# Moving a 31-tap depthwise convolution from between the triangular inverses to beside the in-projection

## What is computed

```python
z = h @ w_in                                             # h: 512 x 1024
c_in, q, k, v, zg, b_raw, a_raw, gate_c, gate_d = split_cols(z, IN_SPLITS)
# convolution branch: 512 channels
u = c_in[..., :CONV_WIDTH] * jax.nn.sigmoid(c_in[..., CONV_WIDTH:])
u = causal_depthwise_conv(u, conv_dw_w) + conv_dw_b      # 31 taps per channel
u = jax.nn.silu(layer_norm(u, conv_ln_gain, conv_ln_bias))
y_conv = u @ w_conv_out
# gated delta branch: 8 heads of 64
qkv = jax.nn.silu(causal_depthwise_conv(concat([q, k, v]), gdn_conv_w))   # 4 taps
...
o = gated_delta_rule(q, k, v, beta, g)   # per head and chunk: a triangular solve, then a scan over chunks
```

## Time and profile before

| | us |
|---|---|
| median of three runs | 974.13 |
| lowest, highest | 972.68, 975.51 |
| the profiled execution's own time | 975.37 |
| its span in the trace | 973.6 |
| PE busy | 852.3 (88%) |
| DVE busy | 644.9 (66%) |
| ACT busy | 491.2 (50%) |
| POOL busy | 357.1 (37%) |

### The profile page before, as it was taken

The page is one execution under the profiler, slowest core; times in us unless marked ns, Lnnn a source line. Parts: engine busy times, 40 slices in busy tenths (PEclk is TensorE's granted clock), DMA queues, the critical chain, the costliest instruction groups (busy, mean ns, idle before and its releaser), DMA issues.

```text
span 973.6 us, 11909 instructions
## 1 busy us (share of the span) xinstructions
PE 852.3 (88%) x4386; PEld 669.7 (69%) x4386; DVE 644.9 (66%) x778; ACT 491.2 (50%) x641; POOL 357.1 (37%) x241
## 2 busy tenths in 40 slices
PE   4999999578868979999999999399999999999950
PEld 3888877478758878885878456267777777777730
DVE  5499424979968964741116212758889888888836
ACT  7555430333424313244532113168888888888832
POOL 6254541575245602212564000223534435343110
PEclk9999999798979969999999998599999999999985
DMA  8563222000000021041080703749999998999406
GB/s 290 194 217 87 87 87 87 1 1 1 1 0 1 1 87 66 21 173 65 23 308 0 279 25 122 278 170 361 353 371 379 364 370 347 351 368 343 169 11 258
DMA packets 49818, 163.53 MB, mean 168 GB/s; under 512 B 11192, under 2 KB 15304, under 8 KB 41198
## 3 DMA queue, kind: packets, MB, share of 16 engines
q1 hardware_dynamic: 42398, 152.41, 41.6%
q0 software_dynamic: 7376, 10.52, 3.2%
HBM read 154.51 MB, written 25.17 MB: 185 GB/s over the span
## 4 chain that ended last, share of the span: by engine, by line
PE 54%; DVE 10%; DMA 2%; ACT 2%; POOL 1%; issue 1%; POOLq 0%; DVEq 0%; SPq 0%; ACTq 0%
PE bank L388 13%; PE bank L390 13%; PE bank L389 13%; PE bank L686 6%; DVE arena L1533 4%; PE bank L731 3%; DVE arena L1584 1%; DMA h_lo<-low_h 1%; DVE arena L1855 1%; PE bank L589 1%; DVE gu_lo L1681 1%; PE bank L627 1%; PE bank L609 1%; PE bank L526 1%; PE bank L753 1%
## 5 line engine op out<-in xcount | busy, mean ns | idle before, releaser
L1681 DVE TENSOR_TENSOR gu_lo<-wgu,gu_hi 128x2048 fp32r<-128x2048 f32 x64 | 146.4, 2289 | 21.8 <-ACT gu_hi L1325 21.5
L986 POOL TENSOR_TENSOR w_lo<-arena,w_hi 128x1024 fp32r<-128x1024 f32 x36 | 89.4, 2490 | 166.0 <-ACT w_hi L1113 166.0
L1325 ACT ACTIVATE gu_hi<-wgu 128x2048 fp32r<-128x2048 f32 x64 | 122.1, 1909 | 19.0 <-DMA h2T_keep<-arena 10.1
L1533 DVE SCALAR_TENSOR_TENSOR arena<-arena 128x512 f32<-128x512 f32 x120 | 123.0, 1089 | 0.1
L999 POOL TENSOR_TENSOR arena<-arena 128x512 f32<-128x512 f32 x56 | 85.3, 1551 | 100.4 <-PE bank L526 41.3
L1069 POOL DMA_INDIRECT arena<-h_rows,row_idx x32 | 81.1, 2534 | 105.4 <-DVE row_idx L1752 88.6
L388 PE MATMUL bank<-h_hi,w_hi 128*128 128x512 f32 x288 | 116.3, 404 | 1.6 <-DMA h_lo<-low_h 1.6
L389 PE MATMUL bank<-h_lo,w_hi 128*128 128x512 f32 x288 | 114.1, 396 | 0.0
L390 PE MATMUL bank<-h_hi,w_lo 128*128 128x512 f32 x288 | 113.9, 396 | 0.0
L1075 POOL DMA_INDIRECT y_rows<-arena,row_idx x32 | 40.2, 1257 | 182.0 <-ACT arena L1364 182.0
L388 PE MATMUL bank<-gu_hi,heT_hi 128*96 128x512 f32 x256 | 103.4, 404 | 2.4 <-DVE heT_lo L1776 1.9
(11 more groups left out here) (298 smaller groups left out, 1647.7 us busy)
## 6 DMA issues: line engine op xcount, KB each, us to landing
wgu<-in_w_expert_gate_dram SPq DMA_DIRECT2D x32, 1024.0 KB, 9.1
wgu<-in_w_expert_up_dram SPq DMA_DIRECT2D x32, 1024.0 KB, 17.7
wd<-in_w_expert_down_dram SPq DMA_DIRECT2D x32, 1024.0 KB, 13.4
arena<-in_w_in_dram SPq DMA_DIRECT2D x8, 2048.0 KB, 8.5
arena<-in_x_dram SPq DMA_DIRECT2D x8, 512.0 KB, 7.1
y_rows<-arena SPq DMA_DIRECT2D x8, 512.0 KB, 9.9
arena<-in_w_in_dram SPq DMA_DIRECT2D x4, 1024.0 KB, 8.2
arena<-in_w_out_dram SPq DMA_DIRECT2D x2, 2048.0 KB, 10.2
```

Source lines behind the costliest of these rows:

```text
L986: gp.tensor_tensor(as_raw(w_lo[pslot(s)], s), raw(s), as_raw(w_hi[pslot(s)], s).bitcast(F32), ALU.subtract)\
L1325: act.activation(gu_hi[j % 2][:, :, ks, :], wgu[j][:, :, ks, :], ACT.Copy)\
L1533: ins = STT(out=acc[:, i, :], in0=upad[:, i, t:t + T], scalar=par[:, o + t:o + t + 1], in1=acc[:, i, :], op0=ALU.mult, op1=ALU.add)
L1681: TT(gu_lo[j][:, :, ks, :], wgu[j][:, :, ks, :], gu_hi[j % 2][:, :, ks, :].bitcast(F32), ALU.subtract)\
```

## The change

The two glu chunks come first in the load table, and PE projects the convolution branch before k. DVE then issues taps from there on: 8 after each of the last three gated blocks, 5 behind each of the twelve short convolutions, 3 (not 5) behind each of the first four heads, 4 (not 9) after each level of the first group, and the last 6 in the second group; none is left for the scan. The four channel blocks are taken two at a time: blocks 0 and 1 through all 31 taps, then 2 and 3, each instruction depending on the one two before it. The first zg piece moves ahead of the transposes of v. The slot numbers on ACT and POOL follow the new chunk order.

```diff
-        chunks = [("k", ...), ("q", ...), ("v", ...), ("glu0", None), ("glu1", None), ("zg", ...),
+        chunks = [("glu0", None), ("glu1", None), ("k", ...), ("q", ...), ("v", ...), ("zg", ...),
...
# PE
+            for f in range(CF):
+                proj("glu0", 2 * f, ("ca", f), ("glu_ready", f + 1), "glu_mm")
+                proj("glu0", 2 * f + 1, ("cb", f), ("glu_sig", f + 1), "glu_mm")
             for f in range(NP):
                 proj("k", f, ("qkv", f), ("pad_ready", f + 1), "qkv_mm")
...
-            for f in range(CF):
-                proj("glu0", 2 * f, ("ca", f), ("glu_ready", f + 1), "glu_mm")
-                proj("glu0", 2 * f + 1, ("cb", f), ("glu_sig", f + 1), "glu_mm")
-            for p in range(NP):
-                wait(pe, "silu_ready", 2 * NP + p + 1)
-                tok_tr(vT, p, ("vtok", p), ("vtok_ready", p + 1), "vtok_tr")
...
+            zg_piece(0)
+            for p in range(NP):
+                wait(pe, "silu_ready", 2 * NP + p + 1)
+                tok_tr(vT, p, ("vtok", p), ("vtok_ready", p + 1), "vtok_tr")
...
-                        for i in ((0,), (1, 2), (), (3,))[h]:
+                        for i in ((1,), (2,), (), (3,))[h]:
                             zg_piece(i)
# POOL: the scaling of k for the state update now stands after slot 19, as before after slot 15
-            for s in range(NPC, 4 * NPC):
+            for s in range(NPC, 5 * NPC):
                 lo_part(s)
...
# ACT
-                hi_part(f + NSL)
+                hi_part(2 * CF + f + NSL)
...
+            for i in range(CF):          # now ahead of the short convolutions' copies
+                src = ready(act, ("cb", i))
+                if i >= 2:
+                    act.wait_ge(S["glu_ready"], i - 1)
+                tell(act.activation(sgl[i % 2], src[:], ACT.Sigmoid), "glu_sig")
+                for j in range(2):
+                    hi_part(2 * i + j + NSL)
...
# DVE
-            taps = [(t, i) for t in range(TAPS) for i in range(CF)]
+            taps = [(t, i) for pair in range(CF // 2) for t in range(TAPS) for i in (2 * pair, 2 * pair + 1)]
...
-                        v.wait_ge(S["dw_step"], n_tap[0] - CF + 1 if t < TAPS - 1 else n_tap[0])
+                        v.wait_ge(S["dw_step"], n_tap[0] - 1 if t < TAPS - 1 else n_tap[0])
...
+            for i in range(CF):
+                src = ready(v, ("ca", i))
+                v.wait_ge(S["glu_sig"], i + 1)
+                tell(TT(upad[:, i, TAPS - 1:], src[:], sgl[i % 2], ALU.mult), "glu_ready")
+                if i > 0:
+                    v.wait_ge(S["glu_ready"], i + 1)
+                    dw(8)
             conv(0)
+            dw(5)
...
             for f in range(1, NP):       # and the same behind the other eight
                 conv(f)
+                dw(5)
...
                     if grp == 0:
-                        dw(5)
+                        dw(3)
...
-                    dw(9 if lv < LV - 1 else 2)
+                    dw(4 if lv < LV - 1 else 2)
```

More of the change, by code:

```diff
@@ L289, in hybrid_layer @@
         win = a["w_in"][0].rearrange("(p k) n -> p k n", k=KT)
-        chunks = [("k", win[:, :, C_K:C_K + VD]), ("q", win[:, :, C_Q:C_Q + VD]), ("v", win[:, :, C_V:C_V + VD]),
-                  ("glu0", None), ("glu1", None), ("zg", win[:, :, C_ZG:C_ZG + VD]),
+        chunks = [("glu0", None), ("glu1", None), ("k", win[:, :, C_K:C_K + VD]), ("q", win[:, :, C_Q:C_Q + VD]),
+                  ("v", win[:, :, C_V:C_V + VD]), ("zg", win[:, :, C_ZG:C_ZG + VD]),
                   ("gc0", win[:, :, C_GC:C_GC + HALF]), ("gc1", win[:, :, C_GC + HALF:C_GC + D]),
@@ L995, in _ @@
                     .then_inc(S["kdec_ready"], 1)
-            for s in range(4 * NPC, FIRST_GATE):
+            for s in range(5 * NPC, FIRST_GATE):
                 lo_part(s)
@@ L1182, in _ @@
             act.activation(nq, ssq, ACT.Sqrt, scale=float(DK), bias=epsb64).then_inc(S["norms"], 1)
[L1184 to L1190, removed]
             def gbc(h):
@@ L1444, in _, with dw @@
             tell(v.tensor_copy(par, ready(v, "par")[:, 0:par.shape[1]]), "setup_ready")
+            taps = [(t, i) for pair in range(CF // 2) for t in range(TAPS) for i in (2 * pair, 2 * pair + 1)]
+            n_tap = [0]
+            def dw(n):
+                for _ in range(n):
+                    if not taps:
+                        return
+                    t, i = taps.pop(0)
+                    o = i * NS
+                    if t == 0:
+                        ins = TS(acc[:, i, :], upad[:, i, 0:T], par[:, o:o + 1], par[:, o + TAPS:o + TAPS + 1], ALU.mult,
+                                 ALU.add)
+                    else:
+                        v.wait_ge(S["dw_step"], n_tap[0] - 1 if t < TAPS - 1 else n_tap[0])
+                        ins = STT(out=acc[:, i, :], in0=upad[:, i, t:t + T], scalar=par[:, o + t:o + t + 1],
+                                  in1=acc[:, i, :], op0=ALU.mult, op1=ALU.add)
+                    if t == TAPS - 1:
+                        ins.then_inc(S["dw_done"], 1)
+                    else:
+                        ins.then_inc(S["dw_step"], 1)
+                        n_tap[0] += 1
             def conv(f):
@@ L1506, in _ @@
             link(v.reciprocal(rq, nq))
-            v.wait_ge(S["consts"], 7 + CF)
-            for i in range(CF):
-                src = ready(v, ("ca", i))
-                v.wait_ge(S["glu_sig"], i + 1)
-                tell(TT(upad[:, i, TAPS - 1:], src[:], sgl[i % 2], ALU.mult), "glu_ready")
             for p in range(NP):
```

19 lines of the change are left out of this document (1 added, 18 removed).

## The result

| | before | changed |
|---|---|---|
| median | 974.31 us (972.68 to 975.51, 4 runs) | 987.89 us (987.04 to 989.61, 4 runs) |
| profiled execution, its span | 975.37, 973.6 | 988.14, 986.3 |
| mean granted TensorE clock | 0.927 | 0.922 |

The ratio is 1.0143, 95% interval 1.0122 to 1.0163: slower, by 13.6 us. The forecast was 989.0 in a range of 973 to 999.

What follows compares the result with a forecast made beforehand. PE was taken to bound the projections and DVE the levels, with DVE limiting the in-projection after the change. Terms of +46.7, -17.3 and -14.7 summed to +14.7 us, giving 989 us from a 974.13 median; range 973 to 999.

Steps and rivals of the forecast that it cites:

- Step 1: Start of conv(0): eight projections come first, and DVE is late with eight taps and three low-part collisions; +50.4 us.
- Step 9: Loads: glu chunks come in two transfers, covered by the small beta and decay product before the first projection; 0 us.
- Step 2: conv(0) start to conv(11) end: 55 taps add 36.9, decay wait shrinks 4.5, one more low-part collision 2.1; +34.5 us.
- late copies of ACT: In-projection: pad copies late in ACT's stream delay DVE; 1 us in each of twelve blocks gives 1001 us; chance 0.08.
- low parts mostly miss the taps: Up to conv(11): POOL's low parts come while DVE waits or reads PSUM, half the price paid; about 969 us; chance 0.13.
- Step 3: End of conv(11) to first decay difference: taps, norms and scaling of v take 10.8 us, 38.55 before; -27.7 us.
- Step 4: First decay difference to first first_inverse: 16.2 us plus 2.8 for PE's half-clock start, 23.0 before; -4.0 us.
- the rival of a low clock throughout: Before the heads: both zg pieces and the products between run at half clock; +9 us, about 998; chance 0.08.
- Step 5: first_inverse(0) to first X product: fewer taps give -2.6, the last block's three taps take 5.7, -3.8; -6.5 us.
- Step 6: Group 0, first D to next group's first difference: PE's 8.89 us sets each level's pace; -17.3 us.
- Step 7: Group 1, first D to reload of the low input part: levels at PE's pace, 44.1 us, 58.75 before; -14.7 us.
- Step 8: Scan: ten taps fewer, but they had cover; 0 us, or -6.7 with the cover gone.

Runs made afterwards that it cites:

- experiment 7: The changed kernel with its two convolution chunks fetched in runs of 1 KB on either side instead of 512 B; 983.47 us, ratio 1.0101.
- order_only: The changed kernel's new chunk order with the taps put back in their old places; 981.93 us, ratio 1.0085.
- Experiment 3: Kernel no_read: the changed kernel with POOL writing zeros for the low parts of weights before the gates instead of computing them; 960.62 us, ratio 0.9856.
- experiment 2: The changed kernel with the 60 taps behind the short convolutions taken to the levels and the scan; 955.98 us, ratio 0.9811.
- experiment 6: POOL's output-gate scaling moved behind group 0's last level: changed kernel 985.76 us; old chunk order, taps where DVE idled, four per scan step, 933.71 us.
- few_taps: The kernel spread with 0, 2 and 3 taps behind levels 1 to 3 of group 0 instead of 5, ten moved behind the last scan step; 934.16 us.
- spread: Old chunk order, taps where DVE idled, four per scan step; against that, POOL's low parts and gate scaling spread one piece per group 0 level; 934.61 us.

## Why the prediction was right, point by point

- **Step 1** (+50.4, measured +52.6): the eight projections and the three collisions behind the last gated block came as counted (11.81 us for eight taps). The excess is the first projection, 2.1 us late (27.48 for 25.39).
- **Step 9** (loads, 0): PE's first projection did start 2.1 us late, but not for the chunk: experiment 7 found the same late start in kernels with the old chunk and an early one in order_only. What I left out is that the small product ahead of it, the cover that I named, can itself run at half clock.
- **Step 2** (+34.5, measured +31.7): right in kind; DVE busy 37.43 of 38 us, conv(11) within 0.6 us of its place. The step itself came out 2.8 lower. DVE's busy time between the two points rose from 62.70 to 99.24 us, 36.5, and its idle time fell from 10.3 to 5.4: so the taps (36.9) and the shorter wait (4.5) were sized right, and the one further collision (2.1) did not come. With 5.4 us of idle time in 104.7, late copies of ACT, a rival of the prediction, played no part. Experiment 3 confirms the price of a low part, experiment 2 that the taps have hardly any cover. The rival by which low parts mostly miss the taps is out.
- **Step 3** (10.8 us from conv(11) to the difference): measured 10.1.
- **Step 4** (19.0 us to first_inverse): measured 20.5, nearer than its parts. The terms named add up to 15.5 and not to the 16.2 in the text. PE's half-clock start of twelve matmuls (176.25 us) fell on the first zg piece, where nothing waited for it; in this stretch it was six matmuls (202.83 to 205.47), 1.3 us where I had 2.8. What the sum left out is the rest of the first head's own products: from the difference to the first of the two pieces it took 3.6 us (1.9 before), with the clock low there too (2.07 us for the eight matmuls at 197.12). PE idled 16 us in one piece and 37 in all from 143 to 200 us; the clock came back within both pieces, so the rival of a low clock throughout is out.
- **Step 5** (-6.5): measured -11.5. The last tap block took 3.09 us, not 5.7, and its first_inverse 1.75 (2.82 before, behind a block of 9.51), because POOL's masks of level 1 waited for PE's last zg product until 236.25 us. I had carried over the collision of the earlier trace rows without asking when the masks could start. That is 3.7 of the 5.0 us; another 0.9 is PE, which before came out of a wait of 11.55 us and began the X products at half clock (4.46 us to the first D, 3.58 now).
- **Step 6** (-17.3): measured -14.2. I gave POOL's scaling of the gates 1 us; it cost 3.6 in level 3, and 0.8 in level 2, where four taps beside the masks and the scaling took 6.48 us and the subtraction followed without a wait. With the scaling moved both levels fell to 8.9 us (experiment 6).
- **Step 7** (-14.7): measured -15.1. **Step 8** (scan, 0): +0.7.

Of the signs that I named, DVE was busy 123.05 of the 130 us from 60 to 190 us, 94.7% and not over 95, and two levels were longer than 9.3 us; conv(0), conv(11), the gap of PE and the reload came within 4 us of their places.

The sum was 14.7 us and the spans differ by 12.7. The total is nearer than its terms: the errors of steps 5 and 2 (-5.0 and -2.8) were met by those of step 1 and of steps 6 and 4 (+2.2, +3.1, +1.5). The mechanism was right; that 989 came within 1.2 us of the measured 987.9 is in part luck.

## What to carry to other kernels

Before moving filler work out of a stage because its engine is the limit there, sum that engine's work in the stage it goes to, with the collisions: here DVE had 30 us free from 105 to 143 us, but none once the taps, the short convolutions and the low parts were in one place. What went with the faster kernels was a quota for each gap (5 taps to a level, 4 to a scan step, 8 behind a gated block), each no longer than the other engine's own pace. And POOL's work beside DVE's counts for both: moving it moves the collision.

## What was not expected of the hardware

- Collisions on SBUF slow both sides. POOL's four masks took 4.96 us in few_taps where no tap ran, and up to 6.83 in spread beside taps.
- A POOL write without reads (MEMSET, 0.95 us) cost DVE's taps nothing, but a TENSOR_SCALAR beside it took 0.92 us in place of 0.48 (no_read, 96.25 us).
- At the start of the program the same product ran at full clock or partly at half from one kernel's profile to the next (granted 0.57 to 0.68, or 1.00, from 20 to 24 us), 2 us of the total that go with no edit here.
- Runs of 512 B in SBUF made the 1 MB loads at the program's start slower: median 10.6 us from issue to landing (10.6 or 10.7 in the five kernels with short runs), 9.8 in the one with runs of 1 KB on either side. The time did not follow (experiment 7).
- A short wait of PE in each scan step seems to cost more than the wait: the granted clock was 0.80 with eight taps in the step and 1.00 with four, over 30 us of the same stage. But with the same four taps it was 0.90 in spread, so not all of it need be the taps'.
